# Gathering an expert's tokens straight into turned form, with the token rows held in TensorE and the selection streamed

## The chip, the cores and the metric

The kernel runs on one core of a Trainium2 chip. The metric is device time in microseconds (us) of one execution; lower is better.

## The reference, cut to what matters

One decoder layer over 256 tokens of width 1024: two attention mixers, then a mixture of 32 experts in which each token goes to its four best. The part that the change touches is the input of an expert, `xb = x_rows[expert]`:

```
h = rmsnorm(x, ln_ffn_g)                       # 256 x 1024
logits = h @ w_router + b_router
top_val, top_idx = lax.top_k(logits, 4)
x_rows = xt[row_tok]                           # the tokens of one expert, one row each
def expert_block(xb, e):
    g = xb @ w_gate[e] + b_gate[e]
    u = xb @ w_up[e] + b_up[e]
    g = minimum(g, 7);  u = clip(u, -7, 7)
    a = g * sigmoid(1.702 * g) * (u + 1)
    return a @ w_down[e] + b_down[e]
y = segment_sum(y_rows * row_p, row_tok)
x = x + y;  return rmsnorm(x, ln_final_g)
```

Each expert has three matrices of 1024 x 1024 float32, 4 MB (MiB) each; 32 experts are 384 MiB.

## The kernel before, in words

**Stages.** The first 235 us or so are the two mixers, the residual and the router. Then comes the loop over the experts, written out as 16 pairs (`pair(i)`, the last one `last_pair()`); expert n = 2i + side. An expert has 64 slots, so its input is 64 x 1024. (A second loop, for experts with more than 64 tokens, is there too and runs as often as the data ask for.)

**Weights.** Each matrix comes in two pieces of 2 MiB, so six pieces per expert, 192 in all. SyncE issues them in one queue into a ring of ten slots: piece n is issued when piece n - 10 has been multiplied (semaphore `pieces_used`). Which slot is which buffer can be seen in the profile as wg, wu, wd, attn, slot_wv, slot_gt, slot_xh. The last piece comes in three parts.

**TensorE's order in one expert n** (each step is one helper, in this order; the source order is the engine's order):
- `product(0, n, G)`: the gate product. A bias matmul (L928, full 128 columns of the array), then for each of 8 slices of the contraction two matmuls of 64 stationary columns (x_g) by 512 streamed weights (L941). The two write different halves of the partitions and run side by side in the array. The traces call this shape `128*64`, and one that uses all columns `128*128`.
- `gather(n + 1)` (L872), the tokens of the next expert: `sel` (128 tokens x 64 slots, a 0/1 matrix times the norm's factor) is held, and the token rows `xs` are streamed, 512 at a time: 2 token blocks x 2 halves, four matmuls of shape 128*64.
- on even sides `turn_selection` (two transposes, L624) for the pair before.
- `product(1, n, U)`: the up product (again L928, then L941).
- `turn_gathered(n + 1)` (four transposes, L624): the gathered rows `x_rows` are turned so that the width lies on the partitions.
- `combine` (L963): half of the weighted sum of the pair before, from pair 1 on.
- `turn_activation(n)` (four transposes, L624), which waits for `a_rows` from VectorE; then a wait for ScalarE's copy `a_t`.
- `down(n)`: the down product (L941). At pair 6 `down_biases` and at pair 8 `residual_in` (L887) follow it.

**Between gather and product.** The gathered rows go from PSUM bank X to `x_rows` by a ScalarE copy (L553), are turned back into bank X by TensorE (L624), and go to `x_g` by a VectorE multiply with the norm's gain (L1345). That multiply stands in VectorE's order behind the work on u (L1357, L1360).

**every_fourth.** The weights are loaded so that a partition holds four rows in a row (RUN = 4). The contraction is therefore dealt out in steps of four, and a turned slice is every fourth element of a row, 16 bytes apart:

```
def every_fourth(ap, r):
    return ap[:, :].rearrange("p (c r) -> p r c", r=RUN)[:, r, :]
```

A float32 matmul is recorded as two instructions, each with its own weight load; a transpose as one.

Of the kernel before, what the change touches and what calls it, by code (L numbers as in the profile page):

```python
# [18 lines left out]
P = 128  # L19
D = 1024  # L20
KT = D // P
SEQ = 256
# [89 lines left out]
def layer(nc, x, ln_mix_g, w_in, b_gate_a, b_gate_b, w_o_a, w_o_b, w_out, ln_ffn_g, w_router, b_router,  # L112
# [6 lines left out]
    def sem(name):  # L119
        return ctx.enter_context(nc.semaphore(name))  # L120

    with ctx:
# [62 lines left out]
        def every_fourth(ap, r):  # L185

            return ap[:, :].rearrange("p (c r) -> p r c", r=RUN)[:, r, :]

        x_rows, g_act, sig = work[:, 1792:2304], v_tok[:, 1, 768:1280], attn[:, 24 * SEQ:26 * SEQ]
        a_rows = nc.alloc_sbuf_tensor_at("a_rows", [P, 512], F32, offset=rows_at)[:]  # L190
        u_act = a_rows
        y_bufs = [attn[:, 0:D], attn[:, D:2 * D]]
# [74 lines left out]
        pieces_used = sem("pieces_used")  # L267
        pick_ready = sem("pick_ready")
        first_sel = sem("first_sel")
        sel_ready, gathered, x_rows_ready = sem("sel_ready"), sem("gathered"), sem("x_rows_ready")  # L270
        xg_turned, xg_ready = sem("xg_turned"), sem("xg_ready")
        g_ready, sig_done, act_ready = sem("g_ready"), sem("sig_done"), sem("act_ready")
        sel_step, g_step, u_step, selp_step = sem("sel_step"), sem("g_step"), sem("u_step"), sem("selp_step")
        a_turned, a_t_ready, y_ready = sem("a_turned"), sem("a_t_ready"), sem("y_ready")
# [159 lines left out]
        def _(act):  # L434
# [113 lines left out]
                act.wait_ge(sel_turned, pairs)  # L548
                act.activation(sel_t, ps[:, bank, 0:SEQ], ACT.Copy).then_inc(sel_t_ready, 1)

            def gathered_out(n):
                act.wait_ge(gathered, n + 1)
                act.activation(x_rows, ps[:, X, :], ACT.Copy).then_inc(x_rows_ready, 1)  # L553

            def turned_activation(n, dst=a_t):
                act.wait_ge(a_turned, n + 1)

# [10 lines left out]
            def pair(i, first=False):  # L568
                for side in range(2):
                    n = i * 2 + side  # L570
                    if side == 0 and first:
                        act.wait_ge(prob_turned, 1)
                        act.activation(prob_t, ps[0:E, DN, 0:SEQ], ACT.Copy).then_inc(prob_t_ready, 1)
                    item_sigmoid(n)
                    gathered_out(n + 1)
                    if side == 0 and not first:
                        turned_selection(i)
                    turned_activation(n)
                    item_out(n, side, y_bufs[i % 2])

            def last_pair():
                item_sigmoid(LAST)
                gathered_out(LAST + 1)
                turned_selection(E // 2 - 1)
                turned_activation(LAST)
                item_sigmoid(LAST + 1)
                turned_selection(E // 2, bank=X)
                turned_activation(LAST + 1, x_g)
                act.wait_ge(pieces_used, FIRST[LAST, 2] + 2)
                for h in range(2):  # L590
                    act.activation(y_bufs[1][0:SLOTS, 512 * h:512 * h + 512], ps[SLOTS * h:SLOTS * h + SLOTS, DN, :], ACT.Copy)\
                       .then_inc(y_ready, 1)
                act.wait_ge(pieces_used, FIRST[LAST + 1, 2] + 2)
                act.activation(y_bufs[1][SLOTS:P, 0:512], ps[0:SLOTS, U, :], ACT.Copy).then_inc(y_ready, 1)

            gathered_out(0)
            pair(0, first=True)
            for i in range(1, E // 2 - 1):
                pair(i)
# [3 lines left out]
            with act.If(count > 0):  # L603
                with act.Fori(0, count) as k:
                    n = k + E
                    gathered_out(n)
                    item_sigmoid(n)
                    turned_activation(n)
                    item_out(n, 0, y_bufs[0])
                    turned_selection(k + (E // 2 + 1))  # L610
# [10 lines left out]
        def _(pe):  # L621
# [246 lines left out]

            def gather_block(b):

                for h in range(2):
                    mm = pe.matmul(ps[SLOTS * h:SLOTS * h + SLOTS, X, :], sel[:, b, :],  # L872
                                   xs[:, b, 512 * h:512 * h + 512], start=(b == 0), stop=(b == NB - 1),
                                   skip_group_check=True)
                if b == NB - 1:
                    mm.then_inc(gathered, 1)

# [30 lines left out]
            def turn_rows(bank, rows_ap):  # L908
                for j in range(4):
                    mm = turn(ps[:, bank, P * j:P * j + P], every_fourth(rows_ap, j))  # L910
                return mm

            def turn_gathered(n):
                pe.wait_ge(x_rows_ready, n + 1)
                turn_rows(X, x_rows).then_inc(xg_turned, 1)

            def turn_activation(n):
                pe.wait_ge(act_ready, n + 1)
# [48 lines left out]

            pe.wait_ge(first_sel, 2)
            gather_block(1)
            turn_gathered(0)  # L970

            def pair(i, first=False):
                for side in range(2):
# [13 lines left out]
                    if side == 0 and first:  # L987
                        pe.wait_ge(tab_ready, 1)
                        pe.matmul(ps[:, Y + 2, 0:33], ones[0:E, :], tab[:, 0:33], start=True, stop=True).then_inc(tab_done, 1)
                    turn_gathered(n + 1)  # L990
                    if not first:
                        combine(i, P, y_bufs[(i - 1) % 2], bs=(side,), first=(i == 1))
                    turn_activation(n)
# [13 lines left out]
            def last_pair():  # L1007
                i = E // 2 - 1
                product(0, LAST, G, x_g)
                gather(LAST + 1)  # L1010
                turn_selection(i, i * 4)
                product(1, LAST, U, x_g)
                turn_gathered(LAST + 1)
                combine(i, P, y_bufs[(i - 1) % 2], bs=(0,))
                turn_activation(LAST)
                pe.wait_ge(a_t_ready, LAST + 1)
                product(0, LAST + 1, G, x_g)
                product(1, LAST + 1, U, x_g)
                combine(i, P, y_bufs[(i - 1) % 2], bs=(1,))
                turn_selection(E // 2, 2 * E, bank=X)  # L1020
                turn_activation(LAST + 1)
                product(2, LAST, DN, a_t, bias=False)
                pe.wait_ge(a_t_ready, LAST + 2)
                product(2, LAST + 1, U, x_g, bias=False)
# [9 lines left out]
            with pe.If(count > 0):  # L1034
                with pe.Fori(0, count) as k:
                    n = k + E
                    gather(n)
                    turn_gathered(n)
                    product(0, n, G, x_g, again=k)
                    product(1, n, U, x_g, again=k)  # L1040
                    turn_activation(n)
                    pe.wait_ge(a_t_ready, n + 1)
                    down(n, again=k)
                    turn_selection(k + (E // 2 + 1), n * 2 + 2)
                    combine(k + (E // 2 + 1), SLOTS, y_bufs[0])
# [3 lines left out]
        def _(dve):  # L1049
# [264 lines left out]

            pick_biases(0)

            gain = cols[:, 24:32].rearrange("p (h j a) -> p j h a", h=2, a=1).broadcast_to([P, 4, 2, SLOTS])
            rstd_b = stat[:, 14:16].rearrange("p (b a) -> p b a", a=1).broadcast_to([P, NB, SLOTS])
            iota_b = iota.rearrange("p (a c) -> p a c", a=1).broadcast_to([P, NB, SLOTS])

# [20 lines left out]
                ins.then_inc(selp_ready, 1)  # L1341

            def gathered_out(n):
                dve.wait_ge(xg_turned, n + 1)
                dve.tensor_tensor(x_g.rearrange("p (h j) c -> p j h c", h=2),  # L1345
                                  ps[:, X, :].rearrange("p (j h c) -> p j h c", h=2, c=SLOTS),
                                  gain, ALU.mult).then_inc(xg_ready, 1)

            def gate_part(n, used):
                dve.wait_ge(pieces_used, used)  # L1350
# [146 lines left out]
```

## Time and profile before

| | |
|---|---|
| median of 3 runs | 1157.78 us (1157.35 to 1160.8) |
| the profiled execution's own time | 1160.92 us |
| its span, first to last instruction | 1158.7 us |
| TensorE (PE) busy | 1089.3 us, 94% |
| VectorE, ScalarE busy | 295.7 us, 202.6 us |
| bytes moved | 439.52 MB, mean 379 GB/s |

An instruction of PE is counted as busy from its start to a modelled end, so the ends of a group overlap the next group by some 0.15 to 0.2 us; the chain of waits gives the same work without that overlap, and it is what is added up below. PEld is the load of the operand that is held. In a shape such as `128*64 128x512` the first part is the tile of the array, the second what is streamed.

### The profile page before, as it was taken

Reading aid. Unit: us, or ns where it says so; the run is one execution under the profiler, and the core shown is the slowest. Engines: PE = TensorE matmul, PEld = TensorE weight load, DVE = VectorE, ACT = ScalarE, POOL = GpSimd, SP = SyncE. Lnnn points to the kernel's source line nnn. Section 1 sums busy time; section 2 is a strip of 40 time slices with the busy share of each in tenths; the row PEclk is TensorE's granted clock in tenths of the full one; section 3 lists DMA queues with packets and bytes.
Section 4 is the critical chain, followed back from the end, with each engine's and each line's share of the span. In section 5 each row is a group of like instructions: output and inputs, shape, how many; then the busy total and the mean of one; then the engine's idle time right before and its main releaser. Section 6 shows DMA issues by size and latency. Waiting matters only on the chain.

```text
span 1158.7 us, 11999 instructions
## 1 busy us (share of the span) xinstructions
PE 1089.3 (94%) x5194; PEld 493.0 (43%) x5194; DVE 295.7 (26%) x674; ACT 202.6 (17%) x349; POOL 4.5 (0%) x11
## 2 busy tenths in 40 slices
PE   7999999999999999999999999999999999999897
PEld 5888888533333333333333333333333333333332
DVE  6656765231111111121111111111111111111112
ACT  4444553111111111111111111111111111101002
POOL 0000000000000000000000000000000000000000
PEclk9999999999999999999999999999999999999999
DMA  9745136999999999999999999999999999999995
GB/s 352 257 135 192 71 113 269 409 361 407 429 428 426 430 426 428 428 428 428 426 429 426 427 429 426 429 427 427 428 427 428 427 429 426 428 429 426 429 428 204
DMA packets 44713, 439.52 MB, mean 379 GB/s; under 512 B 3930, under 2 KB 5362, under 8 KB 20084
## 3 DMA queue, kind: packets, MB, share of 16 engines
q1 hardware_dynamic: 44644, 438.74, 90.9%
q8 instruction: 42, 0.69, 0.2%
q14 instruction: 11, 0.09, 0.0%
q10 hardware_dynamic: 16, 0.00, 0.0%
HBM read 437.68 MB, written 1.05 MB: 379 GB/s over the span
## 4 chain that ended last, share of the span: by engine, by line
PE 63%; DMA 32%; DVE 2%; issue 2%; ACT 1%; SPq 0%; POOL 0%; DVEq 0%; ACTq 0%
PE ps L941 37%; DMA wd<-in_w_up_dram 8%; DMA wu<-in_w_up_dram 7%; DMA attn<-in_w_down_dram 4%; DMA slot_xh<-in_w_up_dram 4%; DMA slot_wv<-in_w_up_dram 4%; PE ps L624 4%; DMA wg<-in_w_up_dram 4%; PE ps L963 3%; PE ps L872 3%; PE ps L822 2%; PE ps L662 2%; PE ps L687 2%; PE ps L654 2%; PE ps L928 1%
## 5 line engine op out<-in xcount | busy, mean ns | idle before, releaser
L1351 DVE TENSOR_SCALAR v_tok<-ps 128x512 f32<-128x512 f32 x32 | 22.1, 692 | 505.3 <-PE ps L941 505.3
L941 PE MATMUL ps<-wd,o_t 128*64 128x512 f32 x608 | 138.3, 596 | 9.7 <-DMA wd<-in_w_up_dram 3.1
L941 PE MATMUL ps<-wu,o_t 128*64 128x512 f32 x608 | 137.7, 602 | 8.9 <-DMA wu<-in_w_gate_dram 3.5
L941 PE MATMUL ps<-wg,o_t 128*64 128x512 f32 x608 | 135.8, 596 | 7.5 <-DMA wg<-in_w_gate_dram 2.3
L941 PEld LDWEIGHTS ps<-wu,o_t 128*64 128x64 f32 x608 | 44.3, 138 | 90.0 <-issue 78.5
L941 PEld LDWEIGHTS ps<-wd,o_t 128*64 128x64 f32 x608 | 43.2, 137 | 90.4 <-issue 77.0
L941 PEld LDWEIGHTS ps<-wg,o_t 128*64 128x64 f32 x608 | 43.2, 137 | 88.1 <-issue 77.3
L941 PE MATMUL ps<-attn,o_t 128*64 128x512 f32 x320 | 73.1, 598 | 6.8 <-ACT o_t L558 2.9
L941 PE MATMUL ps<-slot_wv,o_t 128*64 128x512 f32 x320 | 72.5, 594 | 4.5 <-DMA slot_wv<-in_w_gate_dram 3.4
L941 PE MATMUL ps<-slot_gt,o_t 128*64 128x512 f32 x304 | 69.4, 598 | 5.3 <-issue 2.2
L565 ACT ACTIVATE attn<-ps 64x512 f32<-64x512 f32 x60 | 35.5, 592 | 218.8 <-PE ps L941 218.1
L558 ACT ACTIVATE o_t<-ps 128x512 f32<-128x512 f32 x32 | 19.1, 597 | 307.2 <-PE ps L624 307.1
L941 PE MATMUL ps<-slot_xh,o_t 128*64 128x512 f32 x304 | 68.8, 594 | 3.0 <-DMA slot_xh<-in_w_gate_dram 2.3
L545 ACT ACTIVATE attn<-v_tok 128x512 f32<-128x512 f32 x32 | 20.2, 630 | 242.2 <-DVE v_tok L1351 242.2
L963 PE MATMUL ps<-attn,o_t 128*128 128x512 f32 x128 | 60.3, 594 | 0.8 <-DVE attn L1419 0.8
L872 PE MATMUL ps<-xs,work 128*64 128x512 f32 x256 | 60.7, 593 | 0.2 <-DVE work L1287 0.2
L624 PEld LDWEIGHTS ps<-cst,work 128*128 128x128 f32 (+1 forms) x262 | 32.4, 174 | 47.3 <-issue 38.8
L1357 DVE TENSOR_SCALAR a_rows<-ps 128x512 f32<-128x512 f32 x32 | 22.1, 692 | 113.7 <-PE ps L941 113.7
L624 PE MATMUL ps<-cst,work 128*128 128x128 f32 (+1 forms) x262 | 46.3, 297 | 4.9 <-DVE work L1183 4.2
L941 PEld LDWEIGHTS ps<-slot_wv,o_t 128*64 128x64 f32 x320 | 23.4, 137 | 51.1 <-issue 41.3
L941 PEld LDWEIGHTS ps<-slot_xh,o_t 128*64 128x64 f32 x304 | 22.1, 137 | 47.1 <-issue 39.2
L941 PEld LDWEIGHTS ps<-attn,o_t 128*64 128x64 f32 x320 | 22.4, 136 | 45.2 <-issue 41.7
(167 smaller groups left out, 1081.4 us busy)
## 6 DMA issues: line engine op xcount, KB each, us to landing
wg<-in_w_up_dram SPq DMA_DIRECT2D x14, 2048.0 KB, 38.9
wu<-in_w_gate_dram SPq DMA_DIRECT2D x14, 2048.0 KB, 44.4
wd<-in_w_up_dram SPq DMA_DIRECT2D x13, 2048.0 KB, 39.0
wd<-in_w_down_dram SPq DMA_DIRECT2D x13, 2048.0 KB, 42.7
wu<-in_w_down_dram SPq DMA_DIRECT2D x12, 2048.0 KB, 35.5
wd<-in_w_gate_dram SPq DMA_DIRECT2D x12, 2048.0 KB, 38.5
wg<-in_w_gate_dram SPq DMA_DIRECT2D x12, 2048.0 KB, 38.0
wu<-in_w_up_dram SPq DMA_DIRECT2D x12, 2048.0 KB, 37.1
```

The source lines that it names most:

```text
L545: act.activation(sig, g_act, ACT.Sigmoid, scale=ALPHA).then_inc(sig_done, 1)
L565: act.activation(y_pair[SLOTS * side:SLOTS * side + SLOTS, 512 * h:512 * h + 512], ps[SLOTS * h:SLOTS * h + SLOTS, DN, :], ACT.Copy).then_ ...
L624: return pe.transpose(out_ap, in_ap, ident[0:n, 0:n])
L654: mm = pe.matmul(ps[:, bank, 0:n], h_lo[:, b, k, :], w_hi[:, c % 2, k, 0:n], start=False, stop=(last and k == KT - 1))
L662: mm = pe.matmul(ps[:, bank, 0:n], h_hi[:, b, k, :], w_lo[:, c % 4, k, 0:n], start=False, stop=(last and k == KT - 1))
L687: pe.matmul(ps[:, bank, 0:n], h_hi[:, b, k, :], w_hi[:, c % 2, k, 0:n], start=(k == 0), stop=False)
L822: mm = pe.matmul(ps[:, 2 + 2 * b + h, :], mix_t[:, k, P * b:P * b + P], wo[:, k, 512 * h:512 * h + 512], start=(k == 0), stop=(k == KT - 1))
L872: mm = pe.matmul(ps[SLOTS * h:SLOTS * h + SLOTS, X, :], sel[:, b, :], xs[:, b, 512 * h:512 * h + 512], start=(b == 0), stop=(b == NB - 1), ...
L941: mm = pe.matmul(ps[SLOTS * h:SLOTS * h + SLOTS, bank, :], lhs[:, k, :], ring[n % RING][:, r, 512 * h:512 * h + 512], start=(k == 0 and no ...
L963: mm = pe.matmul(ps[:, Y + 2 * b + h, :], sel_t[0:slots, P * b:P * b + P], y_pair[0:slots, 512 * h:512 * h + 512], start=(first and (b, h) ...
L1351: dve.tensor_scalar(g_act, ps[:, G, :], LIMIT, None, ALU.min).then_inc(g_ready, 1)
L1357: dve.tensor_scalar(u_act, ps[:, U, :], LIMIT, -LIMIT, ALU.min, ALU.max).then_inc(u_step, 1)
```

## The change

The four gather matmuls per expert become sixteen: for each token block and each of the eight slices of the width, 128 columns of `xs` (every fourth element) are held and the 64 columns of `sel` are streamed. The result is the expert's input already turned, eight slices of 64 columns in bank X. The ScalarE copy to `x_rows` and the four transposes `turn_gathered` go, with their semaphores; VectorE's multiply by the gain waits for `gathered` and reads the bank in plain order.

```
@@ TensorE
             def gather_block(b):
-                for h in range(2):
-                    mm = pe.matmul(ps[SLOTS * h:SLOTS * h + SLOTS, X, :], sel[:, b, :],
-                                   xs[:, b, 512 * h:512 * h + 512], start=(b == 0), stop=(b == NB - 1),
-                                   skip_group_check=True)
+                for k in range(KT):
+                    mm = pe.matmul(ps[:, X, SLOTS * k:SLOTS * k + SLOTS],
+                                   every_fourth(xs[:, b, 512 * (k // 4):512 * (k // 4) + 512], k % 4), sel[:, b, :],
+                                   start=(b == 0 and k == 0), stop=(b == NB - 1), skip_group_check=True)
                 if b == NB - 1:
                     mm.then_inc(gathered, 1)
-            def turn_gathered(n):
-                pe.wait_ge(x_rows_ready, n + 1)
-                turn_rows(X, x_rows).then_inc(xg_turned, 1)
...
-            turn_gathered(0)
...
-                    turn_gathered(n + 1)
@@ ScalarE
-            def gathered_out(n):
-                act.wait_ge(gathered, n + 1)
-                act.activation(x_rows, ps[:, X, :], ACT.Copy).then_inc(x_rows_ready, 1)
...
-                    gathered_out(n + 1)
@@ VectorE
-            gain = cols[:, 24:32].rearrange("p (h j a) -> p j h a", h=2, a=1).broadcast_to([P, 4, 2, SLOTS])
+            gain = cols[:, 24:32].rearrange("p (k a) -> p k a", a=1).broadcast_to([P, KT, SLOTS])
             def gathered_out(n):
-                dve.wait_ge(xg_turned, n + 1)
-                dve.tensor_tensor(x_g.rearrange("p (h j) c -> p j h c", h=2),
-                                  ps[:, X, :].rearrange("p (j h c) -> p j h c", h=2, c=SLOTS),
-                                  gain, ALU.mult).then_inc(xg_ready, 1)
+                dve.wait_ge(gathered, n + 1)
+                dve.tensor_tensor(x_g, ps[:, X, :].rearrange("p (k c) -> p k c", c=SLOTS), gain, ALU.mult).then_inc(xg_ready, 1)
```

TensorE's order in the expert loop, an even side (pair 1, side 0), before: gate product, gather, turned selection, bias, up product, turned gathered rows, combine, turned activation, down product. Names are out<-streamed,held.

```order
L941 MATMUL ps<-wg,o_t 64x512 x16
L872 MATMUL ps<-xs,work 64x512 x4
L624 MATMUL ps<-cst,work 128x128 x2
L928 MATMUL ps<-bias_tab,pick_bias 128x512
L941 MATMUL ps<-wu,o_t 64x512 x16
L624 MATMUL ps<-cst,work 128x128 x4
L963 MATMUL ps<-attn,o_t 128x512 x2
L624 MATMUL ps<-cst,a_rows 128x128 x4
L941 MATMUL ps<-slot_gt,o_t 64x512 x8
```

The same place after the change (line numbers are lower, since lines were taken out: L863 is the gather, L615 a transpose, L915 the bias, L928 a product, L950 combine).

```order
L928 MATMUL ps<-wg,o_t 64x512 x16
L863 MATMUL ps<-work,xs 128x64 x16
L615 MATMUL ps<-cst,work 128x128 x2
L915 MATMUL ps<-bias_tab_56,pick_bias_58 128x512
L928 MATMUL ps<-wu,o_t 64x512 x16
L950 MATMUL ps<-attn,o_t 128x512 x2
L615 MATMUL ps<-cst,a_rows_57 128x128 x4
L928 MATMUL ps<-slot_gt_55,o_t 64x512 x8
```

Between the gate and the up product four matmuls became sixteen, with `xs` now the held operand; between the up product and combine the four transposes of `work` are gone.

The start of the expert loop on TensorE, before: the first gather in two halves, with a residual and some small matmuls of the router between them, then the transposes, the bias and the first product.

```order
L898 MATMUL ps<-work,cst 128x32
L872 MATMUL ps<-xs,work 64x512 x2
L887 MATMUL ps<-xs,cst 128x512
L903 MATMUL ps<-work,cst 128x32
L905 MATMUL ps<-cst,work 32x1 x2
L872 MATMUL ps<-xs,work 64x512 x2
L624 MATMUL ps<-cst,work 128x128 x4
L928 MATMUL ps<-bias_tab,pick_bias 128x512
L941 MATMUL ps<-attn,o_t 64x512 x8
```

The same place after the change.

```order
L889 MATMUL ps<-work,cst 128x32
L863 MATMUL ps<-work,xs 128x64 x8
L878 MATMUL ps<-xs,cst 128x512
L894 MATMUL ps<-work,cst 128x32
L896 MATMUL ps<-cst,work 32x1 x2
L863 MATMUL ps<-work,xs 128x64 x8
L915 MATMUL ps<-bias_tab,pick_bias 128x512
L928 MATMUL ps<-attn,o_t 64x512 x8
```

Each half of the gather has eight matmuls where it had two, and nothing stands between the second half and the first product but the bias.

## Rows read from the trace of the kernel before

**Rows 1.** The page: busy times, granted clock and DMA rate by slices.

```profile
PE 1089.3 (94%) x5194; PEld 493.0 (43%) x5194; DVE 295.7 (26%) x674; ACT 202.6 (17%) x349; POOL 4.5 (0%) x11
PEclk9999999999999999999999999999999999999999
GB/s 352 257 135 192 71 113 269 409 361 407 429 428 426 430 426 428 428 428 428 426 429 426 427 429 426 429 427 427 428 427 428 427 429 426 428 429 426 429 428 204
```

**Rows 2.** The chain, one expert of each side: start us, us, what.

```profile
603.90 1.72 PE ps L872 x8
605.61 0.43 PE ps L928
...
613.06 0.68 PE ps L624 x4
613.74 1.72 PE ps L963 x4
615.46 0.47 PE ps L624 x4
615.93 0.73 issue
...
634.83 0.37 PE ps L624 x2
635.20 0.24 PE ps L928
```

**Rows 3.** In order of time: VectorE's last work on u, same expert.

```profile
613.83 0.69 DVE L1360 SCALAR_TENSOR_TENSOR a_rows<-a_rows,v_tok 128x512 f32<-128x512 f32 x1
```

**Rows 4.** The chain: combine in two experts of one side, two apart.

```profile
338.21 1.72 PE ps L963 x4
...
392.94 1.72 PE ps L963 x4
```

**Rows 5.** PE in order of time, 722 us to the end: start, us, what [idle before].

```profile
722.25 3.65 PE L941 MATMUL ps<-wu,o_t 128*64 128x512 f32 x16 [0.40 <-DMA wu<-in_w_up_dram]
...
736.52 1.98 PE L887 MATMUL ps<-xs,cst 128*128 128x512 f32 x4
...
1106.59 3.65 PE L941 MATMUL ps<-wg,o_t 128*64 128x512 f32 x16 [0.23 <-DMA wg<-in_w_up_dram]
...
1126.16 3.65 PE L941 MATMUL ps<-wd,o_t 128*64 128x512 f32 x16 [0.83 <-DMA wd<-in_w_up_dram]
...
1141.36 3.65 PE L941 MATMUL ps<-attn,o_t 128*64 128x512 f32 x16 [1.75 <-DMA attn<-in_w_down_dram]
```

**Rows 6.** The chain: transposes of plain and of every-fourth slices, router's matmuls.

```profile
37.00 0.87 PE ps L624 x8
...
221.72 0.95 PE ps L624 x8
...
224.87 1.71 PE ps L841 x16
```

**Rows 7.** Groups by form: busy us, mean ns of one load of 128 columns.

```profile
L624 PEld LDWEIGHTS ps<-cst,xs 128*128 128x128 f32 x16 | 2.3, 206 | 1.0 <-issue 0.9
```

**Rows 8.** The chain at the start of the expert loop, and in expert 0.

```profile
232.06 1.01 PE ps L872 x4
...
234.67 1.10 PE ps L872 x4
...
237.98 7.09 PE ps L941 x32
...
245.54 1.87 PE ps L872 x8
...
257.86 8.78 PE ps L941 x32
```

**Rows 9.** SyncE's queue: the issue of pieces 14 and 15.

```profile
263.24 3.76 SPq L401 DMA_DIRECT2D wu<-in_w_up_dram  x2
```

**Rows 10.** Engines in a stretch of expert 0's down product: granted clock is third from the end.

```profile
258.50:259.00 0.50, 0.50 (x4) 0.30 (x2) 0.00 (x0) 0.00 (x0) 0.00 (x0) 0.50 1.00 426
```

More of the change, by code:

```diff
@@ L187, in every_fourth @@
             return ap[:, :].rearrange("p (c r) -> p r c", r=RUN)[:, r, :]
-        x_rows, g_act, sig = work[:, 1792:2304], v_tok[:, 1, 768:1280], attn[:, 24 * SEQ:26 * SEQ]
+        g_act, sig = v_tok[:, 1, 768:1280], attn[:, 24 * SEQ:26 * SEQ]
         a_rows = nc.alloc_sbuf_tensor_at("a_rows", [P, 512], F32, offset=rows_at)[:]
@@ L269, in layer @@
         first_sel = sem("first_sel")
-        sel_ready, gathered, x_rows_ready = sem("sel_ready"), sem("gathered"), sem("x_rows_ready")
-        xg_turned, xg_ready = sem("xg_turned"), sem("xg_ready")
+        sel_ready, gathered, xg_ready = sem("sel_ready"), sem("gathered"), sem("xg_ready")
         g_ready, sig_done, act_ready = sem("g_ready"), sem("sig_done"), sem("act_ready")
@@ L582, in last_pair @@
                 item_sigmoid(LAST)
-                gathered_out(LAST + 1)
                 turned_selection(E // 2 - 1)
@@ L594, in last_pair @@
                 act.activation(y_bufs[1][SLOTS:P, 0:512], ps[0:SLOTS, U, :], ACT.Copy).then_inc(y_ready, 1)
-            gathered_out(0)
             pair(0, first=True)
@@ L605, in _ @@
                     n = k + E
-                    gathered_out(n)
                     item_sigmoid(n)
@@ L1012, in last_pair @@
                 product(1, LAST, U, x_g)
-                turn_gathered(LAST + 1)
                 combine(i, P, y_bufs[(i - 1) % 2], bs=(0,))
@@ L1037, in _ @@
                     gather(n)
-                    turn_gathered(n)
                     product(0, n, G, x_g, again=k)
```

## The prediction

> **What bounds the kernel now.** I read the page first [rows 1]. TensorE is busy 94% of the span at the full granted clock (2.4 GHz level), and from the tenth of the 40 slices to the last but one the DMA rate stands at 426 to 430 GB/s. Two resources look full, so the page alone does not say which one a longer or a shorter gather meets. The chain of waits does. Up to about 720 us it consists of TensorE work alone: two experts take 392.94 - 338.21 = 54.73 us, so 27.37 per expert [rows 4]. After that TensorE waits for weights. Read there two starts that a landing released: the second up piece of expert 17 (piece 105 of the ring) at 722.25 and that of expert 30 (piece 183) at 1106.59 [rows 5]. 78 pieces in 384.34 us are 4.93 us each, 29.6 per expert. So DMA is the slower of the two by 2.2 us per expert; it has a lead of a full ring when the products begin, and TensorE has eaten the lead by 722 us, where its first wait for DMA stands (0.40 us).
>
> That gives the number on which all hangs, the **slack**: how much TensorE work can be added before TensorE alone sets the end. From 722.25 to 1106.59 TensorE on its own would need 13 x 27.37 = 355.8 us, and 1.72 more for the two residual matmuls after pair 8 (736.52, L887, four instructions of 0.43). The rest, 26.8, is waiting. To it come 0.40 before, and 0.83 and 1.75 on the way to the last down product [rows 5]. Slack: 29.8 us.
>
> **The change part by part.** Durations are from the chain, where no overlap is counted twice.
>
> *The new gather.* 16 matmuls are 32 instructions, each with its own load of 128 columns and only 64 columns to stream. What a stream costs: L872 and L941 stream 512 columns at 0.43 us per pass (1.72 for two blocks, two passes each, two halves side by side [rows 2]), so 64 columns are 0.054. What a load costs: the nearest row is the router, L841, 16 instructions of the same 128-column load with 32 columns streamed, 1.71 us, that is 0.107 each; the stream is too short to set that, so the load does. Transposes of plain slices run at 0.87 / 8 = 0.109, but those of every-fourth slices of the same `xs` at 0.95 / 8 = 0.119 [rows 6], and four in the loop take 0.47, again 0.12 [rows 2]. The new gather holds exactly such slices of `xs`, so I take 0.119: 32 x 0.119 = 3.81 us. The bounds: 0.054 if the loads vanish behind the stream, and 0.206, one whole unoverlapped load of such a slice [rows 7], at the other end.
>
> The Trainium skill, "Advanced Engine Details and Errata", section SBUF Cachelines, says that SBUF is read in lines of 16 bytes and that a new line at every access costs extra. Every-fourth float32 elements are such accesses, and the trace agrees in sign (0.119 against 0.109); the page gives no figure.
>
> *The array's shape.* After a product (shape 128*64) the first matmul of shape 128*128 costs extra. Four turned rows after the up product take 0.68 where the same four take 0.47: a switch of about 0.20. The bias takes 0.43 after the gather and 0.24 after transposes [rows 2]. After the change the switch moves ahead of the gather, and the bias is cheap on both sides.
>
> *Per expert, from pair 1 on.* Odd side, gather and bias: before 1.72 + 0.43 = 2.15, after 0.20 + 3.81 + 0.24 = 4.25, so +2.10. Even side with the turned selection: before 1.72 + 0.37 + 0.24 = 2.33, after 0.20 + 3.81 + 0.24 + 0.24 = 4.49, so +2.16. After the up product the turned rows (0.68) go, but combine now pays the switch (0.20): -0.48. The activation that comes next is ready in time: VectorE's last operation on u ends at 613.83 + 0.69 = 614.52 [rows 3], 1.5 us after the up product (613.06), and combine covers 0.20 + 1.72. What is left is +1.65 per expert, 29 experts (2 to 30): +47.9.
>
> *Experts 0 and 1* have no combine. There `turn_activation` waits for VectorE in any case, so nothing comes back from the removed transposes. Expert 0's gather goes from 1.87 [rows 8] plus its bias to 3.81 plus a cheaper one, +1.9; expert 1's +2.1. Expert 31 gathers nothing.
>
> *The start.* The first half of the first gather grows from 1.01 to 1.90, and the residual behind it saves its switch: +0.7. From the second half to the first product it is 237.98 - 234.67 = 3.31 now: gather, ScalarE copy, transposes, VectorE multiply. Then it is 1.90 + 0.1 + 0.75 = 2.75: -0.55. Net +0.15 [rows 8].
>
> *ScalarE* loses 32 copies, some 19 us, on an engine that is busy 17% [rows 1] and waits before every other step of the loop: worth nothing outside the start. VectorE's multiply stays, and stands behind the work on u as before.
>
> **The sum.** Added on TensorE: 47.9 + 1.9 + 2.1 + 0.15 = 52.0 us. Less the slack of 29.8: **22.2 us later**. Per expert TensorE would need 27.37 + 1.65 = 29.0, just under DMA's 29.6, so it stays the faster of the two, but it no longer eats the ring's lead before the experts run out. DMA's own end moves little. Its queue runs dry last at the issue of piece 14 (263.24 [rows 9]); that issue comes 0.15 + 1.9 later, and so would a finish set by DMA, about 2 us. TensorE's end is later than that by 20, so TensorE sets it. The DMA waits in the chain disappear.
>
> Against the profiled execution's own 1160.92 this is 1183.1, against the median of the runs 1157.78 it is 1180.0. I cannot tell whether the 3.1 us between them lie before 722 us or in the part that DMA sets (there they would be gone), and take the middle: **1181 us**.
>
> **The rivals.**
>
> *The loads run at the plain pace.* The stride counts in a transpose and not in a matmul: 0.107 as in L841. For: L841 is a true matmul in two passes, the 0.119 comes from transposes only. Against: whatever the operand streamed, it is the held one that is strided in both. Some 1024 instructions times 0.012 is 12.3 less: 52.0 - 12.3 - 29.8 = +9.9, so 1169. The Trainium skill, "TensorE: Matmul & The Clock Gate", section LDWEIGHTS, has this rule: a load costs its columns at 1.2 GHz, 107 ns for 128, without a word on stride; by it the sum is this rival's.
>
> *Not slower: DMA still ends it.* If a load of `xs` hides behind the stream before it, the gather costs what it streams, 32 x 0.054 = 1.7 us. TensorE then has less to do per expert than before, all the lead is eaten as now, and the finish follows piece 14, which comes some 1.8 us earlier since the first gather's detour is gone: 1156. The point from which it decides is the pace: the end stays within 3.5 us of before while the added work is below 29.8 + 3.5, which is a pace of 0.101 or less. For: transposes and loads do overlap somewhere in every row. Against: L841 has even less to stream and does not go below 0.107.
>
> *The clock falls.* For a stretch of some 5 us the gather would stream 64 columns in each 0.119 us slot. In expert 0, after transposes and waits, the granted clock stood at 0.50 (1.2 GHz) [rows 10] and the down product took 8.78 us instead of 7.09. If each of 31 gathers brought that, +1.7 each is 52 more: 1233. Against: the router's stretch (L841, 32 columns per load) and all transposes of the mixers ran at the full clock.
>
> *Dearer loads.* A float32 weight load with a stride in two passes is shown by no row. At 0.13 it would be 11 us more, 1192; without any overlap 1024 x 0.087 = 89 more, 1270. No row runs near that.
>
> **How the numbers follow.** Forecast (pace 0.115 to 0.123, 1176 to 1187): 0.60. Plain pace: 0.17. DMA still ends it: 0.07. Clock: 0.05. Dearer loads: 0.09. Another cause: 0.02. The range 1166 to 1190 holds the first two and the cheaper part of the dearer loads. What a measurement of this kernel can tell from no change is 0.3%, 3.5 us: slower is the forecast, the plain pace, the clock and the dear loads, 0.91; the DMA case lies inside the 3.5 us almost wholly, so 0.06 same; 0.03 faster, which would need the first down product at the full clock as well.
>
> **What would show it.** In the profile after, some 1024 gather instructions of shape 128*128, 64 columns streamed, 3.8 us per expert in the chain (3.4 by the plain pace, 1.7 by the DMA case). Two experts 58.0 us apart from combine to combine, and the same late in the run as early, where before it is 54.7 early. Hardly a wait for DMA on TensorE's lines. The last down product starts about 22 us later than 1141.4. The granted clock full in every slice of the loop. The bias 0.24 after the gather, and combine 0.2 dearer at its start. If the last down product still starts on a landing of DMA, the slack or the pace is wrong; if the clock stands at 0.5 after gathers, it is the clock; if the expert takes longer with a gather of 3.8, an instruction behind it has become dearer that I priced as unchanged.

## The result

The changed kernel takes **1350.26 us** (median of 4 runs, 1349.43 to 1352.74) against 1157.57 for the kernel before on the same chip (4 runs, 1155.68 to 1160.80). The ratio is 1.1662, 95% interval 1.1643 to 1.1681. It is slower by 193 us. The forecast was slower by 23, with a range up to 1190.

The sign and the mechanism of the forecast held: TensorE gets more work than its slack against the weight transfers, and sets the end alone. The price of one load did not hold, and a rival held at 0.05, the falling clock, came true beside it. They are about 120 us and 51 us of the result; the rest is what the new form costs at the forecast's own prices.

### The profile page after: what moved, and what is told of

Read it like the earlier page. It is cut to its first block, busy times and chain, and to the rows that moved or that the text cites. A ratio compares the mean times of both kernels' runs of the same rounds, so it can differ in the third digit from the quotient of the medians.

```text
span 1350.5 us, 13247 instructions
## 1 busy us (share of the span) xinstructions
PE 1304.6 (97%) x5834; PEld 713.4 (53%) x5834; DVE 295.9 (22%) x674; ACT 185.2 (14%) x317; POOL 4.5 (0%) x11
## 4 chain that ended last, share of the span: by engine, by line
PE 94%; DVE 2%; issue 2%; ACT 1%; DMA 1%; SPq 0%; POOL 0%; DVEq 0%; ACTq 0%
PE ps L928 53%; PE ps L863 18%; PE ps L950 4%; PE ps L615 3%; PE ps L915 2%; PE ps L813 2%; PE ps L653 2%; PE ps L678 2%; PE ps L645 2%; PE ps L732 1%; PE ps L733 1%; PE ps L734 1%; ACT o_t L553 1%; DMA xs<-in_x_dram 1%; PE ps L718 0%
## 5 line engine op out<-in xcount | busy, mean ns | idle before, releaser
L863 PEld LDWEIGHTS ps<-work,xs 128*128 128x128 f32 x1024 | 241.4, 329 | 24.6 <-issue 24.3
L863 PE MATMUL ps<-work,xs 128*128 128x64 f32 x1024 | 247.6, 419 | 0.1
L928 PE MATMUL ps<-wd,o_t 128*64 128x512 f32 x608 | 145.6, 622 | 4.3 <-issue 2.2
L928 PE MATMUL ps<-wg,o_t 128*64 128x512 f32 x608 | 144.1, 629 | 4.3 <-issue 2.2
L928 PE MATMUL ps<-wu,o_t 128*64 128x512 f32 x608 | 141.4, 619 | 4.3 <-issue 2.9
L928 PEld LDWEIGHTS ps<-wg,o_t 128*64 128x64 f32 x608 | 45.3, 145 | 92.3 <-issue 89.7
L928 PEld LDWEIGHTS ps<-wd,o_t 128*64 128x64 f32 x608 | 44.9, 144 | 90.6 <-issue 87.8
L928 PEld LDWEIGHTS ps<-wu,o_t 128*64 128x64 f32 x608 | 45.1, 143 | 89.3 <-issue 87.6
L928 PE MATMUL ps<-attn,o_t 128*64 128x512 f32 x320 | 83.8, 671 | 4.7 <-ACT o_t L553 3.0
L928 PE MATMUL ps<-slot_gt,o_t 128*64 128x512 f32 x304 | 77.8, 658 | 4.3 <-issue 2.2
L1294 DVE CAST pick_bias<-cst 128x128 fp32r<-128x128 f32 x32 | 7.3, 227 | 328.0 <-PE ps L928 328.0
L928 PE MATMUL ps<-slot_wv,o_t 128*64 128x512 f32 x320 | 72.1, 592 | 0.0
L928 PE MATMUL ps<-slot_xh,o_t 128*64 128x512 f32 x304 | 68.5, 592 | 0.0
L950 PE MATMUL ps<-attn,o_t 128*128 128x512 f32 x128 | 63.2, 617 | 0.8 <-DVE attn L1400 0.8
L928 PEld LDWEIGHTS ps<-attn,o_t 128*64 128x64 f32 x320 | 24.4, 155 | 52.9 <-issue 49.5
L928 PEld LDWEIGHTS ps<-slot_gt,o_t 128*64 128x64 f32 x304 | 22.7, 152 | 48.0 <-issue 45.4
L928 PEld LDWEIGHTS ps<-slot_wv,o_t 128*64 128x64 f32 x320 | 23.5, 137 | 45.2 <-issue 45.2
L928 PEld LDWEIGHTS ps<-slot_xh,o_t 128*64 128x64 f32 x304 | 22.4, 137 | 42.9 <-issue 42.9
```

The lines of the kernel that those rows point to most:

```text
L863: mm = pe.matmul(ps[:, X, SLOTS * k:SLOTS * k + SLOTS], every_fourth(xs[:, b, 512 * (k // 4):512 * (k // 4) + 512], k % 4), sel[:, b, :], ...
L928: mm = pe.matmul(ps[SLOTS * h:SLOTS * h + SLOTS, bank, :], lhs[:, k, :], ring[n % RING][:, r, 512 * h:512 * h + 512], start=(k == 0 and no ...
L950: mm = pe.matmul(ps[:, Y + 2 * b + h, :], sel_t[0:slots, P * b:P * b + P], y_pair[0:slots, 512 * h:512 * h + 512], start=(first and (b, h) ...
```

## The profile after

The page first: the busy times, the granted clock and the DMA rate in 40 slices, and the group of the new gather (busy us, mean ns of one).

```profile
PE 1304.6 (97%) x5834; PEld 713.4 (53%) x5834; DVE 295.9 (22%) x674; ACT 185.2 (14%) x317; POOL 4.5 (0%) x11
...
PEclk9999999788888888888899888888888888888889
...
GB/s 351 203 178 73 156 230 411 188 366 372 371 369 373 373 373 373 371 376 369 374 363 337 333 365 363 360 341 366 364 367 368 371 362 371 370 369 368 370 214 48
...
L863 PEld LDWEIGHTS ps<-work,xs 128*128 128x128 f32 x1024 | 241.4, 329 | 24.6 <-issue 24.3
```

Three things differ from [rows 1]. The DMA rate in the loop is about 370 GB/s instead of 427: the transfers now wait for TensorE, not the other way. PEclk shows 8 in most slices of the loop, where before all are 9. And one load takes a mean of 329 ns. The row by which I had bounded it, an every-fourth slice loaded for a transpose, takes 206 [rows 7]. TensorE's instructions rose by 640 (5834 - 5194): 1024 for the new gather, less 256 (the old gather) and 128 (its transposes). ScalarE's fell by the 32 copies.

The chain of waits for the two experts that answer to [rows 2] (start us, us, what):

```profile
630.44 7.66 PE ps L863 x32
638.10 0.53 PE ps L915
638.63 8.21 PE ps L928 x32
646.84 1.91 PE ps L950 x4
648.75 0.47 PE ps L615 x4
...
672.15 0.43 PE ps L615 x2
672.58 0.43 PE ps L915
673.00 8.09 PE ps L928 x32
```

The gather takes 7.66 us instead of 1.72 (for both experts), and the up product behind it 8.1 to 8.2 instead of 7.02. These two experts are at the cheap end: over all 31 gathers of the loop the up product behind takes 7.9 to 9.2 us. The dearest is this one:

```profile
745.85 9.21 PE ps L928 x32
```

Combine pays 0.19 for the switch of shape that was forecast (1.91 against 1.72), and its transposes still take 0.47.

Combine in two experts of one side, two apart, early and late in the run, which answers to [rows 4]:

```profile
339.57 1.91 PE ps L950 x4
...
407.98 1.91 PE ps L950 x4
...
1169.20 1.91 PE ps L950 x4
...
1237.47 1.91 PE ps L950 x4
```

(407.98 - 339.57) / 2 = 34.2 us per expert early and 34.1 late. Before it was 27.4 early and 29.6 late. The pace no longer changes within the run: no DMA sets any part of it. The chain at the end says the same. The last two products run without a break, where [rows 5] has waits for weights of 0.83 and 1.75 us.

```profile
1326.38 13.91 PE ps L928 x64
```

TensorE in stretches of 0.5 us around the gather that begins at 630.44 (the columns behind the stretch: sum, busy time and count of L863's matmuls, of its loads, then the granted clock, DMA share, GB/s):

```profile
633.50:634.00 0.50, 0.50 (x4) 0.50 (x3) 1.00 0.92 393
...
634.50:635.00 0.50, 0.50 (x4) 0.50 (x3) 0.50 0.99 426
...
641.00:641.50 0.50, 0.00 (x0) 0.00 (x0) 1.00 0.39 164
```

The clock falls from 1.00 to 0.50 (2.4 to 1.2 GHz) within the gather, some 3.8 us after it began, while TensorE is busy all the time. It comes back 2.4 us into the up product. The count of gather matmuls per 0.5 us is the same on both sides of the fall, so the gather itself does not get dearer; what follows it does. The same holds for all 31 gathers in the chain: each takes 7.66.

The start of the expert loop, which answers to [rows 8], again from the chain:

```profile
238.79 4.01 PE ps L863 x16
...
243.57 9.50 PE ps L928 x32
```

The half gathers take 3.8 and 4.0 us (before 1.01 and 1.10), and the first product starts at 243.57 instead of 237.98 and takes 9.50 instead of 7.09. Here the granted clock is at 0.50 already from about 231.4 us on, in the router's last matmuls and before the first gather, and full again only at 248.5. Not all of that is the change's doing: in experiment 5, whose kernel is the one before up to this point, the clock is at 0.50 from 230.4 to 237.2, and the first product starts at 239.77.

**The budget.** Between the two profiled executions lie 1352.74 - 1160.92 = 191.8 us. Of them:

| term, from the chains | us |
|---|---|
| 31 gathers, 7.66 for 1.72 | +184.1 |
| behind 31 gathers, to the end of the up product (turned selection, bias, product): 279.6 for 233.7 | +45.9 |
| after the up product: 1.91 + 0.47 for 0.68 + 1.72 + 0.47, 29 experts | -14.2 |
| start: first product 5.6 later, and 9.50 instead of 7.09 | +8.0 |
| expert 0's down product at the full clock (7.09 for 8.78) | -1.7 |
| the slack of TensorE before | -29.8 |
| sum | 192.3 |

The sum meets the 191.8 to half a microsecond. The second row is the sum over all 31; before it was 7.45 on 16 of them and 7.63 on 15. At the full clock the new form would take 7.26 and 7.48 there (experiment 7), together 228.4. So the low clock behind the gathers is 279.6 - 228.4 = 51.2 us, and the saved switch at the bias gives back 5.3.

## The experiments

Experiments 1 to 4 ran on one chip with the kernel before at 1158.11 us (7 runs, 1155.97 to 1159.01); experiments 5 to 8 on another with it at 1160.26 (1 run). Experiments 1, 6, 7 and 8 compute something other than the reference (another dealing of the width, another operand streamed, or half of the tokens left out); they are there for their times. Line numbers are those of each kernel.

**Theories.** A: the held operand's stride sets the pace. Every fourth float32 lies in its own 16 bytes, and a true float32 matmul pays for it at each load. B: the new form is dear in itself (32 loads of 128 columns), or the load collides with the weight transfers. C: how much of the 193 us is the clock, and does it fall because of the stride or because of the few columns streamed? D: is the slack of 29.8 right?

### 1. Contiguous slices held

```
-   every_fourth(xs[:, b, 512 * (k // 4):512 * (k // 4) + 512], k % 4), sel[:, b, :],
+   xs[:, b, P * k:P * k + P], sel[:, b, :],
```

> The changed kernel with one edit: the sixteen gather matmuls hold 128 neighbouring columns of xs (128k to 128k+127) in place of every fourth. Same count and shapes; it computes another dealing of the width than the reference's. Theory A (the stride of the held operand makes the load of a true float32 matmul twice as long as that of a transpose): the load falls to the router's 0.107 us, the gather from 7.66 to 3.4 us, and the time to about 1167 us, since 39.7 us of added TensorE work stand against 29.8 of slack. Rival B (the form itself is slow: a narrow stream with a full load behind it, or the steady weight DMA beside it, whatever the stride): the gather stays at 7.7 us and the time at 1350. If it falls to 3.4 us and the clock still drops after it, the time is 1185 to 1205.

Measured: 1179.04 us (1 run). The chain, same stretch:

```profile
627.84 3.72 PE ps L863 x32
...
631.84 7.02 PE ps L928 x32
```

One edit of the address, the same number of instructions, and 171 us are gone, the clock's part with them. The gather takes 3.72 with its switch of 0.2, 0.110 us per instruction. The expected 3.4 us had no switch in it and the router's 0.107, and the expected 1167 us is missed by 12: 31 times 0.3 us are 10 of them. The clock is 1.00 and the up product 7.02 to 7.04 behind every gather of the loop; the start has it low, from 231.6 to 245.3:

```profile
237.00:238.00 1.00, 1.00 (x6) 1.00 (x6) 0.16 (x1) 0.00 (x0) 0.00 (x0) 0.50 0.84 360
...
600.00:700.00 100.00, 97.89 (x480) 43.13 (x480) 16.12 (x36) 8.00 (x14) 0.00 (x0) 1.00 1.01 427
```

(Stretch, sum, then busy time of PE, PEld, DVE, ACT, POOL; the granted clock is third from the end.) The form with its 32 loads is unchanged and the gather is cheap, so B's first half falls. The DMA runs at 427 GB/s beside these loads and does not slow them; whether it slows strided ones is left to experiment 5.

The low clock at the start shows something about contiguous loads. The second half of the first gather, 16 instructions, runs in it:

```profile
236.86 3.69 PE ps L863 x16
```

Experiment 2 has the same 16 at the full clock in 2.01, the changed kernel with its stride in 4.01 at the low one, and experiment 7 with the same stride in 4.01 at the full one. So contiguous loads cost nearly twice as much at the low clock, almost what strided ones cost.

### 2. The same with the layer's result kept

```
+   def plain(ap): return ap[:, :].rearrange("p (r c) -> p c r", r=RUN)
-   dve.tensor_tensor(xs[:, b, q], xs[:, b, q], ps[...], ALU.add)
+   dve.tensor_tensor(plain(xn[:, b, q]), xs[:, b, q]..., ps[...]..., ALU.add)   # dealt once, when the residual is written
    ...
+   xn[:, b, P * k:P * k + P], sel[:, b, :],                                   # gather: contiguous
+   pe.matmul(..., ident, plain(xn[:, b, 512 * h:512 * h + 512]), ...)         # residual: streamed strided
```

> The changed kernel made to hold contiguous slices with the right result: the residual is written once in dealt order (every-fourth slices side by side) into the buffer xn, and gather, transposes and residual matmuls read it from there; buffers xs, h_t and xn change places so that the ring slot fits. Theory A: gather 3.4 us, time about 1167 us (1163 to 1172), as for the plain slices. Rival B: about 1350. Rival C (the clock follows the gather's low streaming, however short): gather 3.4 but products after it slower, 1185 to 1205.

Measured: 1180.84 us (6 runs, 1175.45 to 1182.81), ratio 1.0205 (1.0188 to 1.0222). Half of the first gather, four residual matmuls (L884) and two whole gathers, from the chain of the profiled run, which took 1175.89:

```profile
234.83 2.01 PE ps L869 x16
...
761.97 3.67 PE ps L884 x4
...
1060.23 3.71 PE ps L869 x32
...
1089.03 3.71 PE ps L869 x32
```

3.71 us each, and 1089.03 - 1060.23 = 28.8 per expert. So this is what the form of the change costs with contiguous slices held, but for one thing. The residual matmuls now stream every fourth element, and that is dear as well: four of them take 3.67 us where the changed kernel, which streams them contiguous, takes 1.91 (at 868.96). All eight together are 3.3 us dearer than contiguous ones at the full clock. The expected 1163 to 1172 is missed. With 0.110 for 0.119 the sum of the prediction gives 52.0 - 9.2 - 29.8 = +13.0, and +16.3 with the residual. This execution is 17.8 above the median of the kernel before on the same chip (15.0 above the profiled one of before, which ran on another), and the median is 22.7 above it. The six runs lie in two groups: 1175.5 and 1175.9 at a mean clock of 0.998, and 1180.7 to 1182.8 at 0.991 or 0.992. Experiment 1, with a mean of 0.991, has its low clock at 231.6 to 245.3 us, where the loop begins, and its first product takes 9.03 instead of 7.09. I take the two groups for that, but no trace of a dearer run of this kernel shows it.

### 3. The gather in two halves, on both sides of the up product

```
-   gather(n + 1)
+   pe.wait_ge(sel_ready, n + 1); gather_block(0)
    ...
    product(1, n, U, x_g)
+   gather_block(1)
```

> The changed kernel with the two halves of a gather apart: token block 0 after the gate product as now, block 1 after the up product, ahead of combine. The same loads with the same stride. It asks what the clock costs: in the changed kernel the granted clock falls to 0.50 some 3.9 us after a gather begins, and the bias and up product behind it take 8.7 to 8.95 us instead of 7.3 to 7.5. If a gather half of 3.8 us is too short for the fall: 31 x 1.45 = 45 us less, about 1305, and the clock 1.00 in the loop. If the clock does not follow the length of the gather: 1345 to 1355.

Measured: 1353.24 us (4 runs, 1349.15 to 1354.63), ratio 1.1677 (1.1651 to 1.1703): nothing won. The chain of one expert from its up product on and, below it, stretches of time (columns as in experiment 1):

```profile
599.29 7.02 PE ps L928 x32
606.31 3.88 PE ps L863 x16
610.19 3.19 PE ps L950 x4
613.38 0.72 PE ps L615 x4
```

```profile
609.00:609.50 0.50, 0.50 (x4) 0.50 (x4) 0.00 (x0) 0.00 (x0) 0.00 (x0) 1.00 0.99 426
...
610.50:611.00 0.50, 0.50 (x2) 0.34 (x1) 0.50 (x2) 0.00 (x0) 0.00 (x0) 0.50 1.16 492
```

Here the first half (3.88 us, from 594.95) spares the product behind it (7.02). The second, behind the product, brings the clock to 0.50, and combine and its transposes pay: 3.19 for 1.91, 0.72 for 0.49. That is what the split saved elsewhere: from the first half to the last transpose it is 19.15 us, in the changed kernel 19.00. This expert is not all of them: in 17 of the 31 the up product behind the first half pays instead (7.8 to 8.7 us), in some both do. The time lies in the range named for a clock that does not follow the length of the gather, and the hope that half a gather brings no fall (1305) is gone.

### 4. The kernel before with its gather issued twice

```
-   for b in range(NB): gather_block(b)
+   for last in (False, True):
+       for b in range(NB): gather_block(b, last)
```

> The kernel before with each gather of the loop issued twice (the second overwrites the first with the same numbers): 31 x 1.72 = 53.3 us more of TensorE work, in the same shape as its neighbours, and no strided load. It tests the slack of 29.8 us that the prediction subtracted. By that sum: 53.3 - 29.8 = +23.5, about 1181 us (1177 to 1185), and no waits for DMA late in the run. If there is no slack: +53, 1211. If DMA sets the end whatever TensorE does: 1158 to 1161.

Measured: 1182.95 us (4 runs, 1180.37 to 1184.80), ratio 1.0223 (1.0206 to 1.0240). The chain shows the doubled gather at its full price:

```profile
622.99 3.43 PE ps L872 x16
```

31 x 1.72 = 53.3 us more work made the kernel 24.8 us slower: a slack of 28.5, against 29.8 worked out from [rows 5]. The time lies in the expected range, no wait for a weight transfer is left on TensorE, and D is settled: the slack was right, to the 1.5 us by which the runs before differ.

### 5. The disputed load by itself

The kernel before, with eight groups of 16 matmuls or transposes behind the last down product, when all weights are there. They write a free bank.

```
+   for k in range(16):
+       pe.matmul(ps[:, X, 0:SLOTS], every_fourth(xs[...], k // 2 % 4), sel[:, 0, :], start=True, stop=True)
+   # and the same with step 1, 2, 8; with 128 columns streamed, step 4 and 1; transposes, step 4 and 1
```

> The kernel before, with eight groups of 16 matmuls put behind the last down product, when no weight DMA is left: held slices with a step of 1, 4, 2 and 8 elements and 64 columns streamed; step 4 and step 1 with 128 columns streamed; then transposes with step 4 and step 1. They write a bank that nobody reads. Read is the pace, and it makes the run some 25 us longer. Theory A (the load of a true float32 matmul is what the step slows, whatever DMA does): 0.107 to 0.110 us per instruction at step 1, 0.239 at step 4 and with 128 streamed columns still 0.239; transposes 0.119 and 0.109. Rival D (steady DMA traffic makes the strided load slow): step 4 here at 0.12. Rival E (a strided load cannot overlap the stream, 0.186 plus what is streamed): 0.239 with 64 columns, 0.29 with 128. By the 16-byte line rule step 2 is as fast as step 1 or nearly, and step 8 as slow as step 4.

Measured: 1198.97 us (1 run), 38.7 above the kernel before on its chip and not the expected 25: by the chain the groups take 40.4 us. The chain:

```profile
1147.11 3.71 PE ps L1033 x32
1150.82 7.51 PE ps L1035 x32
1158.34 6.83 PE ps L1037 x32
1165.16 7.59 PE ps L1039 x32
1172.76 7.48 PE ps L1041 x32
1180.23 3.57 PE ps L1043 x32
1183.81 1.92 PE ps L1045 x16
1185.73 1.75 PE ps L1047 x16
```

| held operand | line | us per instruction |
|---|---|---|
| step 1, 64 streamed | L1033 | 0.116 with the switch, 0.110 without |
| step 4, 64 streamed | L1035 | 0.235 |
| step 2, 64 streamed | L1037 | 0.213, at the low clock (below) |
| step 8, 64 streamed | L1039 | 0.237 |
| step 4, 128 streamed | L1041 | 0.234 |
| step 1, 128 streamed | L1043 | 0.112 |
| transposes, step 4 / step 1 | L1045 / L1047 | 0.120 / 0.109 |

The groups by form show it on the loads (busy us, mean ns of one), step 4 and step 1:

```profile
L1035 PEld LDWEIGHTS ps<-work,xs 128*128 128x128 f32 x32 | 7.5, 329 | 0.0
...
L1033 PEld LDWEIGHTS ps<-work,xs 128*128 128x128 f32 x32 | 3.6, 192 | 0.8 <-issue 0.8
```

The stretches of time give clock and DMA (columns as in experiment 1):

```profile
1150.00:1155.00 5.00, 5.00 (x27) 5.00 (x26) 0.00 (x0) 0.00 (x0) 0.00 (x0) 1.00 0.00 0
...
1160.00:1175.00 15.00, 15.00 (x67) 15.00 (x67) 0.00 (x0) 0.00 (x0) 0.00 (x0) 0.50 0.00 0
```

Here lies the failed step. The same slices of `xs`, held for a transpose, cost 0.120 and for a true float32 matmul 0.235. With 0 GB/s of DMA the load is as dear as in the loop (B's second half falls), and with twice the columns streamed it costs the same, so it is the load. Step 8 costs no more than step 4. The step-2 group fell into the low clock that the step-4 group before it had brought; experiment 6 gives it at the full one. At the low clock, with 0.213 for step 2, a load of step 4 or 8 is only a tenth dearer. It gains nothing from the full clock: 0.235 for step 4, which ran at the full clock until 1155, and 0.237 for step 8, which ran at the low one. With 128 columns streamed (L1041) the same strided loads see the clock come back, at about 1175.9.

### 6. Every second element held

Slices of 128 elements as before, now with step 2, so that two elements lie in each 16 bytes; everything else is the changed kernel.

```
+   xs[:, b, 256 * (k // 2):256 * (k // 2) + 256].rearrange("p (c r) -> p r c", r=2)[:, k % 2, :], sel[:, b, :],
```

> The changed kernel with every second element held in place of every fourth (another dealing of the width than the reference's). If two elements in each 16 bytes are enough for the full pace: gather 3.5 to 3.8 us, time as with plain slices, 1175 to 1181. If the load pays for each skipped element: gather about 5.7 us, time about 1250.

Measured: 1184.62 us (1 run). The chain:

```profile
629.84 3.91 PE ps L863 x32
...
634.04 7.02 PE ps L928 x32
```

Time and gather lie a little above what was expected of full pace (1181 us, 3.8 us) and far from the rival's 1250. (3.91 - 0.20) / 32 = 0.116. Step 2 costs 5% over contiguous, step 4 twice as much, step 8 the same as step 4. The doubling lies between 8 and 16 bytes of distance, which is what A says.

### 7. Strided loads, 128 columns streamed

```
-   mm = pe.matmul(ps[:, X, SLOTS * k:SLOTS * k + SLOTS], every_fourth(...), sel[:, b, :],
+   mm = pe.matmul(ps[:, X, P * (k % 4):P * (k % 4) + P], every_fourth(...), work[:, 0:P],
```

> The changed kernel with 128 columns streamed per load in place of 64 (both token blocks' selections beside each other, into overlapping parts of bank X, so its result is not the reference's). If the load alone sets the pace, the gather stays at 7.66 us while TensorE streams twice the columns in it. It asks about the clock: if it fell because the gather streams little, it falls later or not at all, and the bias and up product behind it take 7.3 to 7.5 us again: about 1310. If the clock falls as before: 1350. If load and stream do not overlap: gather 9.4 us, 1400.

Measured: 1298.64 us (1 run). The page's clock row and the chain:

```profile
PEclk9999999999999999999999999999999999999999
```

```profile
642.29 7.66 PE ps L863 x32
...
650.41 7.02 PE ps L928 x32
```

The gather takes the same 7.66, but the clock stays up, and the up product costs what it did before, 7.02 to 7.04 behind every gather of the loop. (At the start it is low from 231.0 to 234.4 here too.) This answers C. **1350.3 - 1298.6 = 51.6 us is the clock** (54.1 between the profiled executions, and 51.2 by the chains behind the gathers), and 1298.6 - 1179.0 = 119.6 us the stride (31 gathers x 3.94 = 122.1 by the chains). The time is 11 us below the 1310 that was expected. The runs come from different chips, on which the kernel before lay up to 2.7 us apart, and two of the three are single ones; the chains are the surer figures. With twice the columns per load the clock holds, at the same stride and the same pace; so the stride by itself does not bring it down.

### 8. Half the gather

```
-   for b in range(NB): gather_block(b)
+   gather_block(0, whole=True)
```

> The changed kernel with block 0's half of each gather alone in the loop (tokens 128 to 255 are left out, so its result is not the reference's). 3.9 us of strided loads per expert, followed by the bias and a product in the shape of before. Added TensorE work about 47 us against 29.8 of slack: 1175 if a stretch this short does not bring the clock down; 1215 if it does.

Measured: 1224.28 us (1 run), mean clock 0.959. Two experts that follow each other:

```profile
614.95 3.88 PE ps L863 x16
...
619.38 8.56 PE ps L927 x32
...
647.47 3.88 PE ps L863 x16
...
651.63 7.02 PE ps L927 x32
```

The same half gather of 3.9 us is followed by a dear up product in one expert and not in the next. Over the run it is dear behind 25 of the 31 and at 7.0 behind six. Both numbers that were expected are too low, 1215 by 9 us. It shows why experiment 3 could not help: a half gather alone mostly brings the clock down too. What decides between the 25 and the six is not shown.

## Why the prediction was wrong

By its own steps:

- **The slack, 29.8.** Right: 28.5 (experiment 4).
- **The form of the sum.** Right. With the pace measured for contiguous slices it gives +13.0, or +16.3 with the dearer residual matmuls, and the profiled execution of experiment 2 is +17.8 on its chip. With the pace of the changed kernel, the switch of 0.20 taken out since the sum has it already, it gives 22.2 + 1024 x (0.233 - 0.119) + 52 = 191, against 192.7 measured. The 52 is the price that the rival carried.
- **The switch and combine.** Right: 1.91 for 1.72. After the up product -0.49 (forecast -0.48). The bias takes 0.28 where the clock is full (experiment 1, at 631.55; forecast 0.24).
- **The start.** Forecast +0.15. In the changed kernel the first product starts 5.6 later and takes 2.4 more: the load's price and a low clock, which the forecast had full there.
- **The load's pace, 0.119 us. This is the step that failed.** It measures (7.66 - 0.20) / 32 = 0.233, and 0.235 in experiment 5. The error is not one of size within a known range: I had called 0.206 the upper bound, a single load without any overlap, and it was taken from the same transposes. That load takes 329 ns in a true matmul. The transposes of the same slices seemed the nearest row since operand, step and shape were equal; the router was the nearest by operation, and it was contiguous. Both were read as if operation and stride added up (0.107 and +0.012). They do not: the stride adds 0.011 to a transpose and 0.125 to a matmul. I had noted that no row shows a strided float32 load in two passes, and then closed the range with rows of the other kind. It costs 1024 x (0.233 - 0.119) = 117 us by the sum; experiment 7 less experiment 1 gives 120 against a pace of 0.110.
- **The dear loads.** Held at 0.09, with "No row runs near that" against it. The mechanism was this one, a strided float32 load in two passes; the highest price that it named was too low (89 for 117).
- **The clock.** Held at 0.05, priced at 52, came at 51.6. It was treated as independent of the pace, and it was not: with contiguous slices (0.110) and with step 2 (0.116) the up product behind every gather is at 7.0, with step 4 and 64 columns it is not. At the forecast pace of 0.119 the rival would, by these neighbours, not have come true, so its chance hung on the price of the load. The row that spoke against it, the router at the full clock, is weaker than it looked: in the changed kernel and in experiment 5 the clock falls in the router's last matmuls.
- **Not slower: DMA still ends it.** Fell: no wait for a weight transfer on TensorE's lines.

The two rules of the Trainium skill: "Advanced Engine Details and Errata", section SBUF Cachelines, says that at least two accesses to a 16-byte line are needed to hide the memory's latency. The trace agrees at the full clock: step 1 0.110, step 2 0.116, step 4 0.235; step 8, at the low clock, 0.237. I had cited the direction and let the transposes set the size. The Trainium skill, "TensorE: Matmul & The Clock Gate", section LDWEIGHTS, gives a load as its columns over 1.2 GHz, by which 128 columns are 107 ns (an estimate from its formula). The trace agrees for steps 1 and 2 at the full clock (0.110, 0.116), and not for step 4 (0.235), nor for step 2 at the low clock (0.213).

**What stays open.** Why a transpose hardly pays for a stride that doubles a true float32 matmul; and what exactly brings the clock down (experiments 3, 7 and 8 bound it from a few sides only, and in the changed kernel and experiment 5 it falls near 231 us, before any gather). Of the sum for experiment 2 1.5 us are left, which is no more than the runs before differ by. No version of the new gather beat the kernel before; the best with the right result, contiguous, is 2% slower, since the form trades 8 instructions of the old gather and 4 transposes (1.72 + 0.68 us) for 32 (3.72 us, and 0.19 more at combine), while ScalarE's saving (202.6 to 185.2 us busy) lies off the path.

## What to carry to other kernels

Take the price of a load from a row with the same step *and* the same kind of instruction; where no such row exists, the end of the range is open, and a probe behind the last instruction of the kernel gives it for a single run. If a float32 operand is to be held in true matmuls over and over, deal it once so that a slice is contiguous or has a step of two at most; here that took 1350.3 us to 1180.8 (experiment 2). Reckon what the other resource will absorb first (here 28 of 53 us), and do not take the clock as full behind a new stretch on TensorE because it was full before: here the low clock cost 1.65 us behind each gather (51.2 / 31), as much as the whole forecast per expert.

## What the hardware showed that I had not expected

- A float32 matmul that holds every fourth or eighth element takes 0.233 to 0.237 us for each of its two instructions, whether the granted clock is 1.00 or 0.50, with 64 or 128 columns streamed, with DMA at 427 GB/s or at 0. Contiguous it is 0.110 at the full clock; at the low one 16 such instructions take 3.69 us instead of 2.01.
- TensorE's clock fell to 0.50 in a stretch in which it was busy all the time, and did not fall with 128 columns per load at the same pace of loads. That difference is worth 51.6 us.
- Moving half of that stretch elsewhere did not save it: in one expert combine paid 3.19 for 1.91 instead of the product, in 17 of 31 the product still did.
- Streaming every fourth element is dear too: four float32 instructions of 512 columns take 3.67 us instead of 1.91.
- The clock can fall before the changed stretch begins: at 230.4 us in experiment 5, in code that is the kernel before.
